# Alternating convolution taps, and the channel norm moved beside the last gate units, in a three-layer fp32 kernel

## The chip, the cores and the metric

The kernel runs on one core of a Trainium2 chip. The metric is device microseconds for one launch, the median of three runs. One more execution was taken with the hardware profiler; all trace rows are from it. "PE" is TensorE, "DVE" VectorE, "ACT" ScalarE, "SP" the queue that issues the weight loads.

## The reference, cut to what matters

256 tokens of width 2048 pass through two blocks of layers, in fp32. The change touches only the first ("even") layer:

```python
def _conformer_conv(a_val, a_gt, w_dw, b_dw, ln_g, ln_b, w_pw, b_pw):
    u = a_val * jax.nn.sigmoid(a_gt)
    y = lax.conv_general_dilated(u, w_dw[:, None, :], ...) + b_dw      # depthwise, 31 taps, causal
    y = jax.nn.silu(_layernorm(y, ln_g, ln_b))                         # over 1024 channels
    return y @ w_pw + b_pw

def _even_layer(x, norm_g, w_in, b_glu, w_dw, b_dw, ln_g, ln_b, w_pw, b_pw, w_out):
    z = _rmsnorm(x, norm_g) @ w_in
    a_val, a_gt, a_gate, q, k, v, b_gate = _split_cols(z, ...)
    ya = _conformer_conv(...) * jax.nn.silu(a_gate)
    yb = _moba_attention(q, k, v) * jax.nn.silu(b_gate)                # 8 heads, causal, one block of 256
    return jnp.concatenate([ya, yb], axis=-1) @ w_out
```

## The kernel before, in words

Activations lie transposed: channels on partitions, in tiles of 128 channels by 256 tokens. Each matrix is worked off in units of 128 output channels ("narrow" units), or, for `e_v` and `e_out`, in "wide" units that are a quarter of the contraction for 512 output columns. The segments of the first layer, in order: `e_gt`, `e_val`, `e_k`, `e_q`, `e_v`, `e_bgate`, `e_agate`, `e_pw` (8 units each) and `e_out` (16).

Every fp32 weight is split in two parts. For each unit, ACT copies the loaded weight into one of four slots as `w_hi` (L1221, L1218), DVE subtracts it to give `w_lo` (L1821, L1817), and PE multiplies three combinations of hi and lo. So a unit n passes ACT, DVE and PE in this order, through semaphores `hi_ready`, `lo_ready` and `acc_ready`. ACT may write the slot of unit n only when PE has finished n-4. The results are drained with a lag of three: after splitting unit n, ACT drains unit n-3 and DVE posts unit n-3 (for "paired" segments an addition from PSUM, L1854; for `e_val` also the product with the sigmoid that gives `u`, L1859). PE has two result banks, so a paired unit n waits for the post of n-2. SP loads chunks of two units (four for `e_pw`) into a ring of two; a chunk's load waits until DVE has split the last unit of the chunk two earlier.

DVE's instructions are in one fixed order: per unit the split, the post, and then a hook for "beside" work. From `e_val` unit 4 to `e_bgate` unit 3 this hook makes the depthwise convolution (`conv_taps`, L2034): 8 tiles of 31 taps, tile after tile, in groups of eight or seven. Each tap reads and writes the same `conv` tile and waits on the semaphore `conv_tap` for the tap just before it.

Counting `e_bgate` and `e_agate` as units u = 0 to 15, the hooks `e_heads_beside` do the attention: on PE, scores of head u-1 (L784), transposes of head u-3 (L799), values of head u-4 (L789, L790), each after unit u; on DVE, mask and maximum of head u-4 (L2058, L2061), division by the sum for head u-5 (L2068, L2069, `p_ready`); on ACT, the exponentials of head u-4. PE's transposes of head 0 after unit 3 wait for `p_ready`.

After unit 13, PE sums the convolution over channels (`conv_mean`, L826). Behind the last gate unit come, one after another: DVE subtracts the mean (L2096), ACT squares (L1453), PE sums the squares (L834), ACT takes the root (L1456), DVE inverts (L2099) and multiplies (L2101), ACT makes eight `Silu` tiles (L1459), ACT copies the result as its hi part into `h_cat` (`h_round`, L1405) and DVE makes the lo part (`h_rest`, L1990). `h_cat` has 16 tiles and feeds every matmul. `e_pw` reads tiles 8 to 15. Its output `ya` goes to tiles 0 to 7, the attention's output `qe` to tiles 8 to 15, and `e_out` contracts over tiles 0 to 15 in this order.

Of the kernel before, what the change touches and what calls it, by code (L numbers as in the profile page):

```python
# [20 lines left out]
ALU = mybir.AluOpType  # L21
# [42 lines left out]
class Seg:  # L64


    def __init__(self, name, units, kt, staged=False, wide=False):
        self.name, self.units, self.kt, self.staged, self.wide = name, units, kt, staged, wide
        self.paired = staged or name in ("e_k", "e_q", "o_iq", "o_q", "g_c", "x_q", "x_k")
        self.kq = kt // 4  # L70
        self.k0 = 8 if name == "g_out" else 0
        self.per_chunk = 2 if wide else max(2, 2 * KT // kt)
# [144 lines left out]
def build(nc, a, out):  # L217
# [154 lines left out]
    def p_tile(a_):  # L372
# [8 lines left out]
             "ht_hi", "ht_ready", "tiles_read", "hhi_ready", "h_ready", "x_normed", "gain1_loaded", "gain_out_loaded",  # L381
# [24 lines left out]
    H_GROUPS = {"conv": 0, "ya": 2, "qe": 4, "cq": 6, "cq_again": 7, "gate": 8, "gdn": 12, "xattn": 16}  # L406
# [81 lines left out]
    def _(sp):  # L488
# [21 lines left out]
        for g in order:  # L510
            if g.name in ("o_small", "g_ab", "g_out"):
                for k in range(g.chunks):
                    load(g, k // 2, k % 2, False)
                continue
            for b in range(min(2, g.chunks)):
                load(g, 0, b, False)
            if g is order[0]:
                for row in other_tables:
                    load_rows(sp, row, "tables_loaded")
            if g.chunks > 2:  # L520
                with sp.Fori(1, g.chunks // 2) as i:
                    for b in range(2):
                        load(g, i, b, True)
# [128 lines left out]
    def _(pe):  # L652
# [150 lines left out]
        def e_heads_beside(u0):  # L803

            def also(j):
# [16 lines left out]
                if u_ == 13:  # L822
                    pe.wait_ge(sem["conv_tap"], TAPS * CT)
                    pe.wait_ge(sem["masked"], HEADS)
                    for c in range(CT):
                        ins = mm(ps[2][:, 0:T], ones[:], conv[:, c, :], start=(c == 0), stop=(c == CT - 1))  # L826
                    ins.then_inc(sem["conv_mean"], 1)
            return also

        seg("e_bgate", also=e_heads_beside(0))  # L830
        seg("e_agate", also=e_heads_beside(8))
        pe.wait_ge(sem["conv_sq"], 1)
        for c in range(CT):
# [366 lines left out]
    def _(act):  # L1200
# [22 lines left out]
        def drain(g, n, i=None):  # L1223
# [16 lines left out]
            elif g.name == "e_bgate":  # L1240
                act.wait_ge(sem["conv_tap"], TAPS * (CT if j == 7 else CT - 1))
# [196 lines left out]
        def e_heads_beside(u0):  # L1438
            def also(i, b):
                u_ = u0 + 4 * i + b  # L1440
                if 4 <= u_ < 4 + HEADS:
                    exp_step(u_ - 4)
                if 6 <= u_ < 6 + HEADS:
                    h = u_ - 6
                    pt_step(h, pe_pt, ps[4 + h % 2], sem["o_ready"], h)
            return also

        seg("e_bgate", e_heads_beside(0))
        seg("e_agate", e_heads_beside(8))

        act.wait_ge(sem["conv_centred"], 1)
        act.wait_ge(sem["o_ready"], HEADS)
        af(csq[:], conv[:], ACT.Square).then_inc(sem["conv_sq"], 1)  # L1453
        section("e_pw")
        act.wait_ge(sem["conv_var"], 1)
        af(rstd[:], ps[3][:, 0:T], ACT.Sqrt, bias=eps[:], scale=1.0 / CW).then_inc(sem["conv_std"], 1)  # L1456
# [3 lines left out]
        h_round(H_GROUPS["conv"], 2, lambda q: conv[:, 4 * q:4 * q + 4], lambda q: act.wait_ge(sem["conv_silu"], 4 * q + 4), CT)  # L1460

        def ya_round(q):

            h_round(H_GROUPS["ya"] + q, 1, lambda _: ya[:, 4 * q:4 * q + 4],
                    lambda _: act.wait_ge(sem["posted"], S["e_pw"].s0 + 4 * q + 4), 4 * q)

        seg("e_pw", lambda i, b: ya_round(0) if 4 * i + b == 7 else None)
        split_to(S["e_out"].n0 + 1)
        drain_to(S["e_out"].n0)
        ya_round(1)  # L1470
        act.wait_ge(sem["acc_ready"], S["e_pw"].n0 + 8)
        act.wait_ge(sem["o_drained"], HEADS)
        h_round(H_GROUPS["qe"], 2, lambda q: qe[:, 4 * q:4 * q + 4], lambda q: None, CT)
# [327 lines left out]
    def _(dve):  # L1801
# [216 lines left out]
        def conv_taps(tile0):  # L2018

            def also(i, b):  # L2020
                if tile0 < 0 and isinstance(i, int) and i == 0:
                    return
                c = tile0 + i
                if tile0 < 0 and b == 0:
                    dve.wait_ge(sem["posted"], S["e_val"].s0 + 1)
                for tap in range(8 * b, min(8 * b + 8, TAPS)):
                    o = flat(conv[:, bass.ds(c, 1), :])
                    win = flat(u[:, bass.ds(c, 1), tap:tap + T])
                    w = prm[:, bass.ds(c + COL["dw"] + tap * CT, 1)]
                    if tap == 0:  # L2030
                        ins = nc.vector.tensor_scalar(o, win, w, col("b_dw", c), ALU.mult, ALU.add)
                    else:
                        dve.wait_ge(sem["conv_tap"], c * TAPS + tap)
                        ins = stt(o, win, w, o, ALU.mult, ALU.add)  # L2034
# [3 lines left out]

        seg("e_val", conv_taps(-1))
        seg("e_k", conv_taps(1))  # L2040
        seg("e_q", conv_taps(3))
        e_v_taps = conv_taps(5)
# [29 lines left out]
        def e_heads_beside(u0):  # L2072
            taps = conv_taps(CT - 1)

            def also(i, b):
# [7 lines left out]
                if 7 <= u_ < 7 + HEADS:  # L2083
# [3 lines left out]
                    tt(qe[:, h, :], ps[6 + h % 2][:, 0:T], bg[:, h, :], ALU.mult).then_inc(sem["o_drained"], 1)  # L2087
            return also
# [4 lines left out]
        dve.wait_ge(sem["conv_mean"], 1)  # L2093
        ch.link(nc.vector.tensor_scalar(psq[:], ps[2][:, 0:T], 1.0 / CW, None, ALU.mult))
        mean = psq[:].unsqueeze(1).to_broadcast([P, CT, T])
        tt(conv[:], conv[:], mean, ALU.subtract).then_inc(sem["conv_centred"], 1)  # L2096
        section("e_pw")
        dve.wait_ge(sem["conv_std"], 1)
        ch.link(nc.vector.reciprocal(rstd[:], rstd[:]))  # L2099
        dve.wait_ge(sem["conv_centred"], 1)  # L2100
        tt(conv[:], conv[:], rstd[:].unsqueeze(1).to_broadcast([P, CT, T]), ALU.mult).then_inc(sem["conv_normed"], 1)  # L2101
        for q in range(2):
            h_rest(H_GROUPS["conv"], q, conv[:, 4 * q:4 * q + 4], CT)
        seg("e_pw", lambda i, b: h_rest(H_GROUPS["ya"], 0, ya[:, 0:4]) if 4 * i + b == 7 else None)
# [436 lines left out]
```

## Time and profile before

| | us |
|---|---|
| median of 3 runs (2612.84 to 2614.36) | 2613.91 |
| the profiled execution, its own time | 2616.9 |
| its span, first to last instruction | 2615.1 |
| PE busy in the span | 2500.4 (96%) |
| DVE busy | 1642.1 (63%) |
| ACT busy | 1181.6 (45%) |

The span is the part that the trace shows; the execution's own time is 1.8 us more. Busy shares are means over the whole kernel, and a matmul's end is modelled, so a stage must be read by the starts of its instructions and by what an engine waited for. Times in rows are microseconds from the span's start.

### The profile page before, as it was taken

The page shows a single profiled execution, that of the slowest core. Times are in us where ns is not written, and L with a number is a line of the kernel's source. Part 1 is how long each engine was busy: PE and PEld are TensorE (multiplying, and loading weights), DVE is VectorE, ACT ScalarE, POOL GpSimd, SP SyncE. Part 2 cuts the span into 40 slices and gives each one's busy share as a digit, 9 for nine tenths or more (in the row PEclk, how much of TensorE's full clock was granted, in tenths as well). Part 3 has the DMA queues.
Part 4 walks back from the last instruction along what each step waited for, and adds up shares of the span by engine and source line. Part 5 has one row for each costly group of instructions (what it writes and reads, how often), then busy time and mean ns, then how long its engine had stood idle before and what let it go on. Part 6 is the DMA issues. An engine that isn't in the chain of part 4 may idle for free.

```text
span 2615.1 us, 35941 instructions
## 1 busy us (share of the span) xinstructions
PE 2500.4 (96%) x14366; PEld 2181.3 (83%) x14366; DVE 1642.1 (63%) x1941; ACT 1181.6 (45%) x1374; POOL 151.2 (6%) x136
## 2 busy tenths in 40 slices
PE   6999897999998999999999999999999999999998
PEld 6878896898887788988887888888888888888886
DVE  4799746445666578479466544554677657765764
ACT  5333655444455554454235434433555334333433
POOL 0000000000110010000000000000022102210220
PEclk9999998999999999999999999999999999999999
DMA  7444433644333555555006555444455555555544
GB/s 232 161 161 161 161 129 130 210 130 161 121 103 121 187 161 162 192 163 187 7 1 225 189 178 197 158 146 161 161 193 192 192 186 181 181 193 193 193 163 143
DMA packets 341284, 422.91 MB, mean 162 GB/s; under 512 B 14491, under 2 KB 267178, under 8 KB 340394
## 3 DMA queue, kind: packets, MB, share of 16 engines
q1 hardware_dynamic: 338620, 411.66, 47.4%
q0 software_dynamic: 2160, 8.40, 1.0%
q8 instruction: 91, 1.49, 0.2%
q10 hardware_dynamic: 382, 1.11, 0.1%
q14 instruction: 31, 0.25, 0.0%
HBM read 419.05 MB, written 2.10 MB: 161 GB/s over the span
## 4 chain that ended last, share of the span: by engine, by line
PE 84%; DVE 12%; ACT 3%; issue 1%; DMA 1%; ACTq 0%; DVEq 0%
PE ps L678 25%; PE ps L679 13%; PE ps L723 8%; PE ps L725 8%; PE ps L724 8%; DVE conv L2034 4%; PE ps L681 4%; PE ps L682 4%; PE ps L683 4%; DVE w_lo L1821 3%; PE ps L944 3%; DVE w_lo L1817 1%; PE ps L754 1%; PE ps L912 1%; PE ps L885 1%
## 5 line engine op out<-in xcount | busy, mean ns | idle before, releaser
L678 PE MATMUL ps<-h_cat,w_hi 128*128 128x512 f32 x3200 | 1143.7, 402 | 34.1 <-DVE h_cat L1990 14.1
L679 PE MATMUL ps<-h_cat,w_lo 128*128 128x256 f32 x3200 | 900.2, 281 | 0.0
L1821 DVE TENSOR_TENSOR w_lo<-ring,w_hi 128x2048 fp32r<-128x2048 f32 (+2 forms) x282 | 592.1, 2102 | 280.9 <-ACT w_hi L1221 277.8
L678 PEld LDWEIGHTS ps<-h_cat,w_hi 128*128 128x128 f32 x3200 | 603.8, 189 | 191.7 <-DVE w_lo L1821 22.0
L679 PEld LDWEIGHTS ps<-h_cat,w_lo 128*128 128x128 f32 x3200 | 607.3, 190 | 2.1 <-issue 1.9
L1221 ACT ACTIVATE w_hi<-ring 128x2048 fp32r<-128x2048 f32 (+2 forms) x282 | 495.5, 1760 | 118.9 <-PE ps L725 74.8
L1817 DVE TENSOR_TENSOR w_lo<-ring,w_hi 128x2048 fp32r<-128x2048 f32 (+1 forms) x136 | 302.9, 2232 | 232.2 <-ACT w_hi L1218 232.2
L1218 ACT ACTIVATE w_hi<-ring 128x2048 fp32r<-128x2048 f32 (+1 forms) x136 | 252.3, 1862 | 291.2 <-PE ps L725 250.8
L723 PE MATMUL ps<-w_hi,h_cat 128*128 128x512 f32 x704 | 277.5, 394 | 7.7 <-DVE w_lo L1817 4.8
L725 PE MATMUL ps<-w_hi,h_cat 128*128 128x512 f32 x704 | 275.7, 392 | 0.0
L724 PE MATMUL ps<-w_lo,h_cat 128*128 128x512 f32 x704 | 275.5, 391 | 0.0
L681 PE MATMUL ps<-h_cat,w_hi 128*128 128x256 f32 (+2 forms) x928 | 267.8, 289 | 7.1 <-DVE w_lo L1821 6.2
L682 PE MATMUL ps<-h_cat,w_hi 128*128 128x256 f32 (+2 forms) x928 | 263.7, 284 | 0.0
L683 PE MATMUL ps<-h_cat,w_lo 128*128 128x256 f32 (+2 forms) x928 | 263.6, 284 | 0.0
L1235 ACT ACTIVATE stage<-ps 128x256 f32<-128x256 f32 x144 | 55.4, 384 | 429.5 <-PE ps L679 429.5
L681 PEld LDWEIGHTS ps<-h_cat,w_hi 128*128 128x128 f32 (+2 forms) x928 | 174.7, 188 | 12.8 <-DVE w_lo L1821 8.4
L682 PEld LDWEIGHTS ps<-h_cat,w_hi 128*128 128x128 f32 (+2 forms) x928 | 174.7, 188 | 1.3
L683 PEld LDWEIGHTS ps<-h_cat,w_lo 128*128 128x128 f32 (+2 forms) x928 | 174.6, 188 | 1.2
L723 PEld LDWEIGHTS ps<-w_hi,h_cat 128*128 128x128 f32 x704 | 133.2, 189 | 36.4 <-DVE w_lo L1817 5.6
L725 PEld LDWEIGHTS ps<-w_hi,h_cat 128*128 128x128 f32 x704 | 133.1, 189 | 27.8
L724 PEld LDWEIGHTS ps<-w_lo,h_cat 128*128 128x128 f32 x704 | 133.3, 189 | 27.5
L723 PE MATMUL ps<-w_hi,act_cat 128*128 128x512 f32 x352 | 137.0, 389 | 0.0
(381 smaller groups left out, 2482.7 us busy)
## 6 DMA issues: line engine op xcount, KB each, us to landing
ring<-in_w_ffn_up SPq DMA_DIRECT2D x44, 2048.0 KB, 7.9
ring<-in_even_w_in SPq DMA_DIRECT2D x28, 2048.0 KB, 7.9
ring<-in_w_mix_in SPq DMA_DIRECT2D x28, 2048.0 KB, 7.9
ring<-in_w_ffn_down SPq DMA_DIRECT2D x16, 2048.0 KB, 8.0
ring<-in_odd_w_in SPq DMA_DIRECT2D x11, 2048.0 KB, 8.1
ring<-in_even_w_out SPq DMA_DIRECT2D x8, 2048.0 KB, 8.2
ring<-in_odd_w_out SPq DMA_DIRECT2D x8, 2048.0 KB, 8.0
ring<-in_w_mix_out SPq DMA_DIRECT2D x8, 2048.0 KB, 8.0
```

What stands on the lines that cost most here:

```text
L678: mm(o[:, 0:2 * T], whi[slot][:, k, :], flat(cat[:, k]), start=first, stop=False)
L679: ins = mm(o[:, T:2 * T], wlo[slot][:, k, :], cat[:, k, 0, :], start=False, stop=end)
L681: mm(o[:m, 0:T], whi[slot][:, k, 0:m], cat[:, k, 0, :], start=first, stop=False)
L682: mm(o[:m, 0:T], whi[slot][:, k, 0:m], cat[:, k, 1, :], start=False, stop=False)
L683: ins = mm(o[:m, 0:T], wlo[slot][:, k, 0:m], cat[:, k, 0, :], start=False, stop=end)
L723: mm(o[:], cat[:, k, 0, toks], hi, start=first, stop=False)
L724: mm(o[:], cat[:, k, 0, toks], lo, start=False, stop=False)
L725: ins = mm(o[:], cat[:, k, 1, toks], hi, start=False, stop=end)
L1218: af(flat(whi[slot])[:, 0:size], flat(ring[c % RING])[:, u0:u0 + size], ACT.Copy).then_inc(sem["hi_ready"], 1)
L1221: af(whi[slot][:, 0:g.kt, 0:m], chunk(c % RING, g)[:, :, u0:u0 + m], ACT.Copy).then_inc(sem["hi_ready"], 1)
L1817: tt(flat(wlo[slot])[:, 0:size], flat(ring[c % RING])[:, u0:u0 + size], flat(whi[slot])[:, 0:size].bitcast(F32), ALU.subtract).then_inc(se ...
L1821: tt(wlo[slot][:, 0:g.kt, 0:m], chunk(c % RING, g)[:, :, u0:u0 + m], whi[slot][:, 0:g.kt, 0:m].bitcast(F32), ALU.subtract).then_inc(sem["l ...
```

## The change

Taps: `conv_taps` now numbers all 248 taps, and alternates between two tiles (tap 0 of tile 0, tap 0 of tile 1, tap 1 of tile 0, ...). Tap n waits only for tap n-2, the last one on its own tile. The number of taps per unit is 7 in `e_val` (units 4 to 7), `e_k` and `e_q`, 8 in `e_v`, 11 in `e_bgate` units 0 to 3 (before: 8, 8, 8, 7 repeating). The DVE segments `e_val`, `e_k`, `e_q` and ACT's two gate segments are written out instead of looped.

Norm: the channel sum moves from behind unit 13 to behind unit 11, the sum of squares behind unit 12. Subtraction and squares are made by DVE and ACT at their own u = 14, root, inverse and product at u = 15. The `Silu` tiles stand between the drains of `e_agate`'s units 5 and 6, and the hi copies follow PE's last gate unit quarter by quarter (new semaphore `agate_read`), with the `e_pw` weight splits between them. The convolution goes to tiles 0 to 7 of `h_cat`, and `e_pw` waits for each half of them.

Output: `e_out` contracts tiles 8 to 15 first (`k0 = 8`). `qe` is written into `h_cat` in the first units of `e_pw`; both halves of `ya` are written when `e_pw` is over, after three units of `e_out` have been split.

```diff
--- before.py
+++ after.py
@@ -68,7 +68,7 @@
         self.name, self.units, self.kt, self.staged, self.wide = name, units, kt, staged, wide
         self.paired = staged or name in ("e_k", "e_q", "o_iq", "o_q", "g_c", "x_q", "x_k")
         self.kq = kt // 4
-        self.k0 = 8 if name == "g_out" else 0
+        self.k0 = 8 if name in ("e_out", "g_out") else 0
         self.per_chunk = 2 if wide else max(2, 2 * KT // kt)
 
 
...
@@ -403,7 +403,7 @@
         ends[c] = g.n0 + min(g.per_chunk * (j + 1), g.units)
     seg_of_unit = {g.n0 + j: (g, j) for g in order for j in range(g.units)}
     seg_of_narrow = {g.f0 + j: (g, j) for g in order if not g.wide for j in range(g.units)}
-    H_GROUPS = {"conv": 0, "ya": 2, "qe": 4, "cq": 6, "cq_again": 7, "gate": 8, "gdn": 12, "xattn": 16}
+    H_GROUPS = {"conv": 0, "qe": 2, "ya": 4, "cq": 6, "cq_again": 7, "gate": 8, "gdn": 12, "xattn": 16}
     SQUARES = {0: 8, 1: 16, 2: 32, 4: 40, 3: 48, 5: 56, 6: 64}
 
     def width(g, j):
@@ -508,7 +508,7 @@
                 sp.dma_start(chunk(slot, g)[:, :, cols], src).then_inc(loaded[slot], 16)
 
         for g in order:
-            if g.name in ("o_small", "g_ab", "g_out"):
+            if g.name in ("o_small", "g_ab", "e_out", "g_out"):
                 for k in range(g.chunks):
                     load(g, k // 2, k % 2, False)
                 continue
@@ -819,23 +819,23 @@
                     if h >= 2:
                         pe.wait_ge(sem["o_drained"], h - 1)
                     e_values(h, h).then_inc(sem["o_ready"], 1)
-                if u_ == 13:
+                if u_ == 11:
                     pe.wait_ge(sem["conv_tap"], TAPS * CT)
                     pe.wait_ge(sem["masked"], HEADS)
                     for c in range(CT):
                         ins = mm(ps[2][:, 0:T], ones[:], conv[:, c, :], start=(c == 0), stop=(c == CT - 1))
                     ins.then_inc(sem["conv_mean"], 1)
+                if u_ == 12:
+                    pe.wait_ge(sem["conv_sq"], 1)
+                    for c in range(CT):
+                        ins = mm(ps[3][:, 0:T], ones[:], csq[:, c, :], start=(c == 0), stop=(c == CT - 1))
+                    ins.then_inc(sem["conv_var"], 1)
             return also
 
         seg("e_bgate", also=e_heads_beside(0))
-        seg("e_agate", also=e_heads_beside(8))
-        pe.wait_ge(sem["conv_sq"], 1)
-        for c in range(CT):
-            ins = mm(ps[3][:, 0:T], ones[:], csq[:, c, :], start=(c == 0), stop=(c == CT - 1))
-        ins.then_inc(sem["conv_var"], 1)
-        pe.wait_ge(sem["h_ready"], H_GROUPS["conv"] + 2)
-        seg("e_pw", rhs=h_cat[:, CT:])
-        wide_seg("e_out", tiles_ready=H_GROUPS["ya"])
+        seg("e_agate", also=e_heads_beside(8), read="agate_read")
+        seg("e_pw", tiles_ready=H_GROUPS["conv"])
+        wide_seg("e_out", tiles_ready=H_GROUPS["qe"])
         turn_first(1)
         seg("o_small", norm=1)
 
@@ -1238,7 +1238,7 @@
             elif g.name in ("e_k", "e_q"):
                 ins = af({"e_k": ke, "e_q": qe}[g.name][:, at_j, :].rearrange("p a t -> p (a t)"), src, ACT.Copy)
             elif g.name == "e_bgate":
-                act.wait_ge(sem["conv_tap"], TAPS * (CT if j == 7 else CT - 1))
+                act.wait_ge(sem["conv_tap"], 2 * TAPS * (j // 2 + 1))
                 ins = af(bg[:, at_j, :].rearrange("p a t -> p (a t)"), src, ACT.Silu)
             elif g.name == "e_agate":
                 ins = af(ag[:, at_j, :].rearrange("p a t -> p (a t)"), src, ACT.Silu)
@@ -1443,34 +1443,57 @@
                 if 6 <= u_ < 6 + HEADS:
                     h = u_ - 6
                     pt_step(h, pe_pt, ps[4 + h % 2], sem["o_ready"], h)
+                if u_ == 14:
+                    act.wait_ge(sem["conv_centred"], 1)
+                    act.wait_ge(sem["o_ready"], HEADS)
+                    af(csq[:], conv[:], ACT.Square).then_inc(sem["conv_sq"], 1)
+                if u_ == 15:
+                    act.wait_ge(sem["conv_var"], 1)
+                    af(rstd[:], ps[3][:, 0:T], ACT.Sqrt, bias=eps[:], scale=1.0 / CW).then_inc(sem["conv_std"], 1)
             return also
 
-        seg("e_bgate", e_heads_beside(0))
-        seg("e_agate", e_heads_beside(8))
-
-        act.wait_ge(sem["conv_centred"], 1)
-        act.wait_ge(sem["o_ready"], HEADS)
-        af(csq[:], conv[:], ACT.Square).then_inc(sem["conv_sq"], 1)
-        section("e_pw")
-        act.wait_ge(sem["conv_var"], 1)
-        af(rstd[:], ps[3][:, 0:T], ACT.Sqrt, bias=eps[:], scale=1.0 / CW).then_inc(sem["conv_std"], 1)
+        seg("e_bgate", e_heads_beside(0), unrolled=True)
+        seg("e_agate", e_heads_beside(8), unrolled=True)
+
+        agate, pw, e_out = S["e_agate"], S["e_pw"], S["e_out"]
+        split_to(pw.n0 + 1)
+        drain_to(agate.n0 + 6)
         act.wait_ge(sem["conv_normed"], 1)
         for c in range(CT):
             af(conv[:, c, :], conv[:, c, :], ACT.Silu, bias=col("cln_b", c), scale=col("cln_g", c)).then_inc(sem["conv_silu"], 1)
-        h_round(H_GROUPS["conv"], 2, lambda q: conv[:, 4 * q:4 * q + 4], lambda q: act.wait_ge(sem["conv_silu"], 4 * q + 4), CT)
+        drain_to(agate.n0 + 7)
+
+        def conv_round(q):
+
+            act.wait_ge(sem["agate_read"], q + 1)
+            h_round(H_GROUPS["conv"] + q, 1, lambda _: conv[:, 4 * q:4 * q + 4],
+                    lambda _: act.wait_ge(sem["conv_silu"], 4 * q + 4), 4 * q)
+
+        def qe_round(q):
+
+            if q == 0:
+                act.wait_ge(sem["acc_ready"], agate.n0 + 8)
+                act.wait_ge(sem["o_drained"], HEADS)
+            h_round(H_GROUPS["qe"] + q, 1, lambda _: qe[:, 4 * q:4 * q + 4], lambda _: None, CT + 4 * q)
 
         def ya_round(q):
 
+            if q == 0:
+                act.wait_ge(sem["acc_ready"], pw.n0 + 8)
             h_round(H_GROUPS["ya"] + q, 1, lambda _: ya[:, 4 * q:4 * q + 4],
-                    lambda _: act.wait_ge(sem["posted"], S["e_pw"].s0 + 4 * q + 4), 4 * q)
-
-        seg("e_pw", lambda i, b: ya_round(0) if 4 * i + b == 7 else None)
-        split_to(S["e_out"].n0 + 1)
-        drain_to(S["e_out"].n0)
+                    lambda _: act.wait_ge(sem["posted"], pw.s0 + 4 * q + 4), 4 * q)
+
+        split_to(pw.n0 + 2)
+        conv_round(0)
+        split_to(pw.n0 + 3)
+        conv_round(1)
+        section("e_pw")
+        seg("e_pw", lambda i, b: qe_round(4 * i + b - 1) if 4 * i + b in (1, 2) else None)
+        for j in range(3):
+            split_to(e_out.n0 + j + 1)
+            drain_to(pw.n0 + 6 + j)
+        ya_round(0)
         ya_round(1)
-        act.wait_ge(sem["acc_ready"], S["e_pw"].n0 + 8)
-        act.wait_ge(sem["o_drained"], HEADS)
-        h_round(H_GROUPS["qe"], 2, lambda q: qe[:, 4 * q:4 * q + 4], lambda q: None, CT)
         wide_seg("e_out", lambda c: squares(S["e_out"], c))
         section("o_small", 3)
         table_for_roots()
@@ -2015,31 +2038,28 @@
         turned_rows(0, x)
         seg("e_gt", tables_beside, unrolled=True)
 
-        def conv_taps(tile0):
+        def conv_taps(first, per_unit, from_unit=0):
 
             def also(i, b):
-                if tile0 < 0 and isinstance(i, int) and i == 0:
-                    return
-                c = tile0 + i
-                if tile0 < 0 and b == 0:
-                    dve.wait_ge(sem["posted"], S["e_val"].s0 + 1)
-                for tap in range(8 * b, min(8 * b + 8, TAPS)):
-                    o = flat(conv[:, bass.ds(c, 1), :])
-                    win = flat(u[:, bass.ds(c, 1), tap:tap + T])
-                    w = prm[:, bass.ds(c + COL["dw"] + tap * CT, 1)]
+                at = 4 * i + b - from_unit
+                for n in range(first + at * per_unit, min(first + (at + 1) * per_unit, CT * TAPS)) if at >= 0 else ():
+                    two, tap = n // (2 * TAPS), n % (2 * TAPS) // 2
+                    c = 2 * two + n % 2
+                    o, win = conv[:, c, :], u[:, c, tap:tap + T]
+                    w = prm[:, c + COL["dw"] + tap * CT:c + COL["dw"] + tap * CT + 1]
                     if tap == 0:
+                        dve.wait_ge(sem["posted"], S["e_val"].s0 + c + 1)
                         ins = nc.vector.tensor_scalar(o, win, w, col("b_dw", c), ALU.mult, ALU.add)
                     else:
-                        dve.wait_ge(sem["conv_tap"], c * TAPS + tap)
+                        dve.wait_ge(sem["conv_tap"], n - 1)
                         ins = stt(o, win, w, o, ALU.mult, ALU.add)
                     ins.then_inc(sem["conv_tap"], 1)
             return also
 
-
-        seg("e_val", conv_taps(-1))
-        seg("e_k", conv_taps(1))
-        seg("e_q", conv_taps(3))
-        e_v_taps = conv_taps(5)
+        seg("e_val", conv_taps(0, 7, 4), unrolled=True)
+        seg("e_k", conv_taps(28, 7), unrolled=True)
+        seg("e_q", conv_taps(84, 7), unrolled=True)
+        e_v_taps = conv_taps(140, 8)
         g = S["e_v"]
         for j in range(g.units):
             split_to(g.n0 + j + 1)
@@ -2070,7 +2090,7 @@
                ALU.mult).then_inc(sem["p_ready"], 1)
 
         def e_heads_beside(u0):
-            taps = conv_taps(CT - 1)
+            taps = conv_taps(204, 11)
 
             def also(i, b):
                 u_ = u0 + 4 * i + b
@@ -2085,28 +2105,35 @@
                     dve.wait_ge(sem["o_ready"], h + 1)
                     dve.wait_ge(*emptied(S["e_bgate"], h + 1))
                     tt(qe[:, h, :], ps[6 + h % 2][:, 0:T], bg[:, h, :], ALU.mult).then_inc(sem["o_drained"], 1)
+                if u_ == 14:
+                    dve.wait_ge(sem["conv_mean"], 1)
+                    ch.link(nc.vector.tensor_scalar(psq[:], ps[2][:, 0:T], 1.0 / CW, None, ALU.mult))
+                    mean = psq[:].unsqueeze(1).to_broadcast([P, CT, T])
+                    tt(conv[:], conv[:], mean, ALU.subtract).then_inc(sem["conv_centred"], 1)
+                if u_ == 15:
+                    dve.wait_ge(sem["conv_std"], 1)
+                    ch.link(nc.vector.reciprocal(rstd[:], rstd[:]))
+                    dve.wait_ge(sem["conv_centred"], 1)
+                    tt(conv[:], conv[:], rstd[:].unsqueeze(1).to_broadcast([P, CT, T]), ALU.mult)\
+                        .then_inc(sem["conv_normed"], 1)
             return also
 
         seg("e_bgate", e_heads_beside(0), unrolled=True)
         seg("e_agate", e_heads_beside(8), unrolled=True)
 
-        dve.wait_ge(sem["conv_mean"], 1)
-        ch.link(nc.vector.tensor_scalar(psq[:], ps[2][:, 0:T], 1.0 / CW, None, ALU.mult))
-        mean = psq[:].unsqueeze(1).to_broadcast([P, CT, T])
-        tt(conv[:], conv[:], mean, ALU.subtract).then_inc(sem["conv_centred"], 1)
+        pw, e_out = S["e_pw"], S["e_out"]
+        split_to(pw.n0 + 2)
+        h_rest(H_GROUPS["conv"], 0, conv[:, 0:4])
+        split_to(pw.n0 + 3)
+        h_rest(H_GROUPS["conv"], 1, conv[:, 4:8])
         section("e_pw")
-        dve.wait_ge(sem["conv_std"], 1)
-        ch.link(nc.vector.reciprocal(rstd[:], rstd[:]))
-        dve.wait_ge(sem["conv_centred"], 1)
-        tt(conv[:], conv[:], rstd[:].unsqueeze(1).to_broadcast([P, CT, T]), ALU.mult).then_inc(sem["conv_normed"], 1)
+        seg("e_pw", lambda i, b: h_rest(H_GROUPS["qe"], 4 * i + b - 1, qe[:, 16 * i + 4 * b - 4:16 * i + 4 * b], CT)
+            if 4 * i + b in (1, 2) else None)
+        for j in range(3):
+            split_to(e_out.n0 + j + 1)
+            post_to(pw.n0 + 6 + j)
         for q in range(2):
-            h_rest(H_GROUPS["conv"], q, conv[:, 4 * q:4 * q + 4], CT)
-        seg("e_pw", lambda i, b: h_rest(H_GROUPS["ya"], 0, ya[:, 0:4]) if 4 * i + b == 7 else None)
-        split_to(S["e_out"].n0 + 1)
-        post_to(S["e_out"].n0)
-        h_rest(H_GROUPS["ya"], 1, ya[:, 4:8])
-        for q in range(2):
-            h_rest(H_GROUPS["qe"], q, qe[:, 4 * q:4 * q + 4], CT)
+            h_rest(H_GROUPS["ya"], q, ya[:, 4 * q:4 * q + 4])
         wide_seg("e_out", lambda c: add(S["e_out"], c))
         section("o_small", 3)
         add(S["e_out"], 3)
```

## Rows read from the trace of the kernel before

**Rows 1.** Stretches: length, busy us (instructions) of each engine, TensorE's granted clock, DMA share, GB/s.
```profile
40.72:75.28 34.56, 34.56 (x291) 34.56 (x289) 16.23 (x15) 13.64 (x12) 0.00 (x0) 1.00 0.71 232
75.28:97.89 22.61, 22.61 (x131) 19.60 (x129) 15.67 (x23) 8.85 (x8) 0.00 (x0) 1.00 0.43 137
412.44:426.57 14.13, 14.13 (x83) 12.26 (x81) 10.66 (x15) 7.96 (x11) 0.00 (x0) 1.00 0.10 27
454.11:519.39 65.28, 65.28 (x289) 54.05 (x288) 33.31 (x19) 26.67 (x24) 0.00 (x0) 1.00 0.58 196
97.89:269.25 171.36, 159.96 (x834) 133.46 (x832) 164.85 (x258) 59.24 (x50) 0.00 (x0) 1.00 0.49 164
269.25:312.19 42.94, 36.00 (x269) 34.92 (x269) 34.03 (x48) 28.28 (x34) 0.00 (x0) 0.92 0.49 159
389.88:407.43 17.55, 3.44 (x17) 2.67 (x16) 11.03 (x8) 13.13 (x18) 0.00 (x0) 0.74 0.35 120
407.43:454.11 46.68, 43.27 (x200) 36.00 (x201) 28.12 (x30) 21.60 (x22) 0.00 (x0) 0.91 0.37 131
```

**Rows 2.** What PE waited for, 75.28 to 454.11: total us, times, longest.
```profile
PE ps L678 <- DVE h_cat L1990: 14.1, 1, 14.1
PE ps L799 <- DVE pe_p L2069: 6.8, 1, 6.8
...
PE ps L723 <- DVE w_lo L1817: 3.1, 1, 3.1
```

**Rows 3.** Timeline of DVE, `e_val` and `e_k` taps: start, length of the merged group, instruction.
```profile
129.57 0.48 DVE L1859 SCALAR_TENSOR_TENSOR u<-stage,prm,sig 128x256 f32<-128x256 f32 x1
129.97 4.13 DVE L2034 SCALAR_TENSOR_TENSOR conv<-u,prm,conv 128x256 f32<-128x256 f32 x8
134.01 2.28 DVE L1821 TENSOR_TENSOR w_lo<-ring,w_hi 128x2048 fp32r<-128x2048 f32 x1
...
136.55 3.60 DVE L2034 SCALAR_TENSOR_TENSOR conv<-u,prm,conv 128x256 f32<-128x256 f32 x7
```

**Rows 4.** Timeline of DVE, four independent instructions of the tap's kind and shape.
```profile
593.70 1.67 DVE L2128 SCALAR_TENSOR_TENSOR cq<-cq,prm,orq 128x256 f32<-128x256 f32 x4
```

**Rows 5.** Timeline of DVE, the first head: mask, the next split, the division.
```profile
293.49 0.68 DVE L2058 SCALAR_TENSOR_TENSOR pe_p<-ps,causal 128x512 f32<-128x512 f32 x1
...
297.86 2.29 DVE L1821 TENSOR_TENSOR w_lo<-ring,w_hi 128x2048 fp32r<-128x2048 f32 x1 [2.96 <-ACT w_hi L1221]
300.07 0.68 DVE L2058 SCALAR_TENSOR_TENSOR pe_p<-ps,causal 128x512 f32<-128x512 f32 x1
...
301.58 0.69 DVE L2069 TENSOR_TENSOR pe_p<-pe_p,small 128x512 f32<-128x512 f32 x1
```

**Rows 6.** Timeline of PE behind one gate unit: scores, transposes, values, next unit.
```profile
318.03 1.03 PE L784 MATMUL ps<-ke,qe 128*128 128x256 f32 x4
318.90 0.60 PE L799 MATMUL ps<-ident,pe_p 128*128 128x128 f32 x4
319.33 0.60 PE L789 MATMUL ps<-pe_pt,ve 128*128 128x256 f32 x2
...
319.91 0.36 PE L681 MATMUL ps<-h_cat,w_hi 128*128 128x256 f32 x1
```

**Rows 7.** Timeline of DVE and ACT, the channel norm.
```profile
378.86 2.29 DVE L2096 TENSOR_TENSOR conv<-conv,psq 128x2048 f32<-128x2048 f32 x1
...
381.18 1.91 ACT L1453 ACTIVATE csq<-conv 128x2048 f32<-128x2048 f32 x1 [11.61 <-DVE conv L2096]
...
395.89 1.75 DVE L2099 RECIPROCAL rstd<-rstd 128x256 f32<-128x256 f32 x1
...
400.00 4.04 ACT L1459 ACTIVATE conv<-conv,prm 128x256 f32<-128x256 f32 x8 [2.85 <-DVE conv L2101]
...
405.01 2.36 DVE L1990 TENSOR_TENSOR h_cat<-conv,h_cat 128x1024 fp32r<-128x1024 f32 x2 [5.05 <-ACT h_cat L1405]
```

**Rows 8.** The page, part 6, weight loads: KB each, median us to landing.
```profile
ring<-in_even_w_out SPq DMA_DIRECT2D x8, 2048.0 KB, 8.2
```

More of the change, by code:

```diff
@@ L380, in build @@
              "row_ready", "emptied", "squared", "gained", "totalled", "std_ready", "rstd_ready", "scaled_dve", "scaled_act", "turned",
-             "ht_hi", "ht_ready", "tiles_read", "hhi_ready", "h_ready", "x_normed", "gain1_loaded", "gain_out_loaded",
+             "ht_hi", "ht_ready", "tiles_read", "agate_read", "hhi_ready", "h_ready", "x_normed", "gain1_loaded", "gain_out_loaded",
              "conv_tap", "conv_mean", "conv_centred", "conv_sq", "conv_var", "conv_std", "conv_normed", "conv_silu",
```

## The prediction

> **What bounds the kernel now.** I read the stretches with their granted clock first, then PE's waits, then the timelines of DVE, PE and ACT at the places found. The stretches come first, since a matmul's busy time is modelled and only the starts of units tell its pace. Where PE never waits, a unit has a fixed pace [rows 1]: 34.56 us for six unpaired units of `e_gt`, 5.76 each; 22.61 for four paired of `e_val`, 5.65 each; 14.13 for five of `e_pw`, 2.83 each; 65.28 for twelve wide ones of `e_out`, 5.44 each. Those are the first four rows; PE is busy throughout and the clock is 1.00. The other four rows are longer than their units need. From 97.89 to 269.25 PE does 4 + 8 + 8 paired and 8 wide units, 20 x 5.65 + 8 x 5.44 = 156.6, but takes 171.4, with DVE busy 164.9 of it: DVE bounds this stretch. In the next two stretches and the last, PE waits for something that was late: for `pe_p` of the first head (6.8), for `h_cat` of the convolution (14.1), for one `w_lo` (3.1) [rows 2]. Each of those waits is followed by a spell at half clock, seen as 0.92, 0.74 and 0.91 in the stretches. So the first layer is PE's wherever DVE or a serial chain isn't late, and the change aims at all four places. From 454.11 on nothing is changed; the rest moves as a block.
>
> **The price of a tap.** A merged group of eight dependent taps lasts 4.13 us, one instruction 0.485, so the pitch is (4.13 - 0.485) / 7 = 0.52 us; the whole group up to the next start is 134.01 - 129.97 = 4.04, so the last, with nothing dependent behind it, takes 0.40 [rows 3]. Four independent instructions of the same kind and shape last 1.67, a pitch of (1.67 - 0.48) / 3 = 0.40 [rows 4]. They overlap; dependent ones don't, and wait some 0.04 for the semaphore too. With two tiles alternating, tap n needs the end of tap n-2, which started 0.80 earlier and lasts 0.485: satisfied. I take 0.40 a tap; the bounds are 0.40 and 0.52 (no effect). 248 taps x 0.12 = 30 us of DVE time.
>
> The Trainium skill, page "VectorE: DVE Perf Modes", section "The DRAIN you can't avoid", speaks against this: the next op does not start until the pipe is empty and the semaphore costs nothing, so one should cut the number of ops, not the waits. By it the taps would stay at 0.52. The rows above say otherwise for this shape, and I go by them.
>
> **DVE-bound stretch, 97.89 to 269.25.** New DVE time a unit: split and paired post 136.55 - 134.01 = 2.54 [rows 3], 7 taps 2.8, so 5.36 in `e_k` and `e_q` against PE's 5.65: PE is the bound, DVE waits. `e_val` units add the 0.40 of `u` (129.57 to 129.97): 5.76 to 5.9, four times 0.1 to 0.2 over PE's pace, covered by the post's slack (the post of n-3 is due only when PE has finished n-2, a unit later). `e_v`: split 2.21 (297.86 to 300.07, [rows 5]) + 8 x 0.40 = 5.4 against 5.44. The ring: a load needs 8.2 [rows 8] after DVE's split, and its next use is two units (10.9 to 11.3) on, plus DVE's lead; covered, with 3 us to spare, and without cover each chunk would cost what is missing. Saved: 171.4 - 156.6 = **14.8**.
>
> **First head, 269.25 to 312.19.** Five gate units need 28.8, plus scores 0.87, transposes 0.43, values 0.58 [rows 6]: behind u = 1 and 2 scores, u = 3 scores and transposes, u = 4 all three, 2 x 0.87 + 1.30 + 1.88 = 4.9. 33.7 instead of 42.9, if `p_ready` is in time. That is the tight place. While paired units run, DVE's post ties it to PE: split n+1 starts about 3.8 after PE ends n-3 (0.7 for the drain, an estimate from the 0.33 post of the same shape, then 0.33 and 2.8), 13.2 before PE begins n+1. Over `e_v`, with three last posts, DVE takes 44.4 to PE's 43.5: lead 12.3. `e_bgate` units 0 to 3 have eleven taps, 2.21 + 4.4 = 6.6 each: the split of unit 4 starts 14.3 after PE's start of unit 0. From there 2.2 to the mask, 4.4 from mask to the next split (293.49 to 297.86, the exponentials and ACT's copy inside), 2.2 to the next mask, 2.2 to the end of the product [rows 5]: 25.3. PE arrives at 4 x 5.76 + 3 x 0.87 = 25.65. The margin is 0.3 us; each 0.01 on the tap's pitch takes about 1 us (64 + 44 taps where DVE sets the pace). At 0.40 saved: **9.2**; I allow 0.5 for a slip.
>
> **Norm chain, 389.88 to 407.43.** All of the 17.55 goes but the sum of squares, 3.3 on PE (its 3.44 busy), which must be done somewhere: **14.3**. The cover: with zero at the end of unit 11, values and mean end at 3.9; mean copy and subtraction to 6.8, squares (1.9) to 8.8, and PE finishes unit 12 at 3.9 + 5.76 = 9.7, margin 0.9. Sum of squares to 12.9; root, then inverse, product (395.89 to 400.00, 4.1) to 17.8. `Silu` stands behind the drain of unit 13, which PE ends at 18.7: 19.3 + 4.0 = 23.3 [rows 7]. Unit 15 starts at 24.4 and ends at 30.2; hi and lo of the first half (1.0 and 1.2) follow its first quarter, and the `e_pw0` split is long done, so `e_pw` may start at 30.2 with about 2 us in hand; its second half is needed 1.4 later and comes at about 30.7. Behind ACT's waits for the norm stand only splits of `e_pw`, due at 30 or later.
>
> **`e_pw` and the start of `e_out`, 407.43 to 454.11.** 46.7 against 8 x 2.83 + 3 x 5.44 = 38.9: **7.7**, of which 2.2 is `e_pw0` at half clock, 5.0 the late `w_lo` of `e_out1` and the half clock behind it. `e_out0` and 1 now read `qe`, copied during `e_pw`. With zero at the start of `e_pw`, the load for `e_out2` goes out at 14.1, lands at 22.9, is split by 27, posts and both `ya` halves end at 30.4; `e_out2` starts at 33.5. Margin 3 us. The three units' splits are done before `ya`, so the old gap has no successor I can see. ACT and DVE segments written out instead of looped: no cost, as `e_v` and the gates are already so on DVE and show no gaps; a bound above is nothing that a row shows.
>
> **Sum.** 14.8 + 9.2 + 14.3 + 7.7 = 46.0, less 0.5: 45.5. On the profiled execution: 2616.9 - 45.5 = 2571.4, span 2569.6. That execution is 3.0 over the median; on the median 2613.9 - 45.5 = **2568.4 us**.
>
> **Rivals.**
> (a) Head 0 late: a tap's pitch of 0.42 to 0.46, or a slower exponential. PE waits 2 to 7 us at the transposes; waits of 3 us and more were followed by half clock, so 2571 to 2579. For: the margin is 0.3. Against: 0.397 in [rows 4], 0.40 before every split. Chance 0.17.
> (b) Norm or ring late: one of the waits in ACT's or DVE's new order comes late by more than its margin, worst one whole landing (8.2): 2571 to 2578. For: ACT's order is now full of waits for PE. Against: margins of 1 to 3 us. Chance 0.13.
> (c) Alternation gives nothing, pitch 0.52. DVE does the same work to `e_bgate` 3, head 0 is as late as before; only norm and output gain, 22.0: 2592. This is what the page's rule above comes to. Chance 0.05.
> (d) Slower than before: two interleaved streams on different `u` and `conv` tiles make each tap dearer. DVE then pays 248 x (p - 0.52), and the 22 us are eaten at p = 0.61; at 0.65 the time is 2624. No row shows such an instruction over 0.52. Chance 0.02. No change at all would need p at just about 0.61: 0.01.
> The forecast case, 2565 to 2572, has the remaining 0.62.
>
> **How the numbers follow.** 2568 is the likeliest. The range 2564 to 2581 holds the forecast and nearly all of (a) and (b), about 0.9, less what later stages may do (half-clock spells behind 454 fall where they fall, a few us); (c) and (d) are outside. About 0.2% (5 us) is what a measurement here can tell from no change. Faster by more: (forecast), (a), (b), (c): 0.97; within 0.01; slower 0.02.
>
> **What would show it.** Taps of a group at 0.40 from start to start; 156 us from `e_val4` to `e_bgate0`, with no PE wait for `ke`, `qe` or `stage`; transposes of head 0 without a wait; `e_pw0` right behind `e_agate` 7; no half clock between 75 us and `o_small`. PE waits for `pe_p` at 280 us would mean (a), for `h_cat` or `w_lo` at 369 to 410 (b), taps at 0.52 (c). The prediction is wrong if a stage I took for PE's turns out to wait for ACT, whose new order has more waits for PE than any stretch of the profile before.

## The result, and the profile after

The changed kernel takes 2565.74 us (median of 4 runs, 2565.47 to 2569.22), the kernel before 2614.14 (4 runs, 2612.84 to 2614.85). The ratio is 0.9821, 95% interval 0.9809 to 0.9833: 48.4 us saved. The forecast was 2568.4, 45.5 saved, range 2564 to 2581.

The stretches of the changed kernel, cut at the same units as [rows 1]: `e_val4` to `e_bgate0`, to `e_bgate5`, to `e_pw0`, to `e_out0`, to `e_out3`, and from there to the end. Columns: stretch, length, busy us (instructions) of PE, PE's weight loads, DVE, ACT and POOL, granted clock, DMA share, GB/s.

```profile
97.73:254.35 156.62, 156.62 (x835) 134.14 (x834) 153.67 (x265) 61.00 (x52) 0.00 (x0) 1.00 0.56 186
254.35:288.04 33.69, 33.69 (x270) 33.11 (x268) 25.87 (x39) 22.51 (x29) 0.00 (x0) 1.00 0.51 163
288.04:369.00 80.96, 80.96 (x632) 79.14 (x630) 46.59 (x48) 55.55 (x75) 0.00 (x0) 1.00 0.39 131
369.00:391.61 22.61, 22.61 (x131) 19.60 (x129) 19.02 (x24) 13.78 (x18) 0.00 (x0) 1.00 0.55 186
391.61:407.99 16.38, 16.38 (x74) 13.51 (x73) 12.39 (x9) 9.16 (x7) 0.00 (x0) 1.00 0.71 243
407.99:2563.70 2155.71, 2098.19 (x11887) 1821.72 (x11885) 1312.76 (x1494) 966.56 (x1138) 149.08 (x126) 0.99 0.50 162
```

In the first five rows PE's busy time is the length of the stretch and the clock is 1.00. The view of PE's waits from 75 to 410 us, which had the rows of [rows 2] in the kernel before, is empty. Against [rows 1]: 156.6 for 171.4, 33.7 for 42.9, 39.0 (22.61 + 16.38) for 46.7; and `e_agate` 7 ends where `e_pw0` starts. `e_val4` to `e_out3` took 454.11 - 97.89 = 356.2 us and now takes 310.3, 46.0 less.

DVE's timeline in `e_k`, and where the first head begins (`w_lo` is L1844 now, the tap L2055, mask L2078, maximum L2081, product L2089):

```profile
125.48 2.29 DVE L1844 TENSOR_TENSOR w_lo<-ring,w_hi 128x2048 fp32r<-128x2048 f32 x1
127.69 0.41 DVE L1877 TENSOR_TENSOR ke<-ke,ps 128x256 f32<-128x256 f32 x1
128.02 2.86 DVE L2055 SCALAR_TENSOR_TENSOR conv<-u,prm,conv 128x256 f32<-128x256 f32 x7
130.79 2.28 DVE L1844 TENSOR_TENSOR w_lo<-ring,w_hi 128x2048 fp32r<-128x2048 f32 x1
...
263.61 4.44 DVE L2055 SCALAR_TENSOR_TENSOR conv<-u,prm,conv 128x256 f32<-128x256 f32 x11
267.97 2.29 DVE L1844 TENSOR_TENSOR w_lo<-ring,w_hi 128x2048 fp32r<-128x2048 f32 x1
270.17 0.69 DVE L2078 SCALAR_TENSOR_TENSOR pe_p<-ps,causal 128x512 f32<-128x512 f32 x1
...
278.26 0.69 DVE L2089 TENSOR_TENSOR pe_p<-pe_p,small 128x512 f32<-128x512 f32 x1
```

Seven taps last 2.86, a pitch of (2.86 - 0.48) / 6 = 0.397, where [rows 3] had 0.52; a unit takes DVE 5.31 (125.48 to 130.79) against PE's 5.65. The product of head 0 ends at 278.95. PE's timeline there:

```profile
279.10 1.03 PE L784 MATMUL ps<-ke,qe 128*128 128x256 f32 x4
279.96 0.60 PE L799 MATMUL ps<-ident,pe_p 128*128 128x128 f32 x4
```

The transposes start at 279.96, with no wait: the product (278.26 + 0.69 = 278.95) was ready 1.0 us before.

The norm chain after, on ACT (squares L1449, root L1452, `Silu` L1463, hi copies L1405) and on DVE (subtraction L2112, inverse L2115, lo parts L2013):

```profile
345.51 1.92 ACT L1449 ACTIVATE csq<-conv 128x2048 f32<-128x2048 f32 x1 [6.51 <-DVE conv L2112]
...
351.93 0.47 ACT L1452 ACTIVATE rstd<-ps,eps 128x256 f32<-128x256 f32 x1 [1.14 <-PE ps L831]
...
357.96 4.03 ACT L1463 ACTIVATE conv<-conv,prm 128x256 f32<-128x256 f32 x8
...
364.88 1.06 ACT L1405 ACTIVATE h_cat<-conv 128x1024 fp32r<-128x1024 f32 x1
```

```profile
352.44 1.75 DVE L2115 RECIPROCAL rstd<-rstd 128x256 f32<-128x256 f32 x1 [0.89 <-ACT rstd L1452]
...
365.97 1.22 DVE L2013 TENSOR_TENSOR h_cat<-conv,h_cat 128x1024 fp32r<-128x1024 f32 x1
367.12 1.22 DVE L1844 TENSOR_TENSOR w_lo<-ring,w_hi 128x1024 fp32r<-128x1024 f32 x1
368.25 1.22 DVE L2013 TENSOR_TENSOR h_cat<-conv,h_cat 128x1024 fp32r<-128x1024 f32 x1
```

ACT and DVE still wait in this chain, but PE doesn't. The squares end at 347.4, and PE starts its sum of squares (L831) at 348.3, right behind unit 12. The two halves for `e_pw` are ready at 367.2 and 369.5; `e_pw0` starts at 369.0 and needs the second half a unit, 1.4 us, later.

### The profile page after: what moved, and what is told of

The parts are those of the page before. It is cut to its first block, busy times and chain, and to the rows that moved or that the text cites. A ratio compares the mean times of both kernels' runs of the same rounds, so it can differ in the third digit from the quotient of the medians.

```text
span 2563.7 us, 35901 instructions
## 1 busy us (share of the span) xinstructions
PE 2486.2 (97%) x14366; PEld 2175.2 (85%) x14366; DVE 1622.7 (63%) x1941; ACT 1176.6 (46%) x1371; POOL 151.1 (6%) x136
## 4 chain that ended last, share of the span: by engine, by line
PE 94%; DVE 4%; ACT 2%; issue 0%; DMA 0%; ACTq 0%; DVEq 0%
PE ps L678 29%; PE ps L679 15%; PE ps L723 9%; PE ps L725 9%; PE ps L724 9%; PE ps L681 4%; PE ps L682 4%; PE ps L683 4%; PE ps L944 3%; PE ps L754 1%; DVE w_lo L1844 1%; PE ps L912 1%; PE ps L885 1%; PE ps L1141 1%; PE ps L1132 1%; PE ps L901 0%
## 5 line engine op out<-in xcount | busy, mean ns | idle before, releaser
L1844 DVE TENSOR_TENSOR w_lo<-ring,w_hi 128x2048 fp32r<-128x2048 f32 (+2 forms) x282 | 592.3, 2102 | 278.6 <-ACT w_hi L1221 275.6
```

What stands on the lines that cost most here:

```text
L1844: tt(wlo[slot][:, 0:g.kt, 0:m], chunk(c % RING, g)[:, :, u0:u0 + m], whi[slot][:, 0:g.kt, 0:m].bitcast(F32), ALU.subtract).then_inc(sem["l ...
```

## The experiments

**Only the taps, `e1_taps_only`.** The kernel before with the new `conv_taps`, its spread and the written-out segments:

```diff
-        seg("e_k", conv_taps(1))
+        seg("e_k", conv_taps(28, 7), unrolled=True)
...
-                        dve.wait_ge(sem["conv_tap"], c * TAPS + tap)
+                        dve.wait_ge(sem["conv_tap"], n - 1)
```

> Only the alternating taps (with their new spread over the units); norm chain, places in h_cat and order of e_out as before. My theory: the four places are independent, each gives back its own idle time. Taps at a pitch of 0.40, 97.9 to e_bgate0 in 156.6 us, head 0 in time, together 24.0 us: about 2590. The gap behind e_agate 7 stays at 17.5. Rival (the places share a cause, so that an earlier PE only meets the norm chain's wait earlier and longer): the gap behind e_agate 7 grows and less than 20 us is saved.

Measured: 2589.46 us, ratio to before 0.9903 (0.9885 to 0.9921), 25.1 less than before's median of 2614.57 in these runs. Its stretches `e_val4` to `e_bgate0`, to `e_bgate5`, end of `e_agate` 7 to `e_pw0`, and on to `e_out3`:

```profile
97.31:253.93 156.62, 156.62 (x835) 134.03 (x833) 153.70 (x265) 61.02 (x52) 0.00 (x0) 1.00 0.56 186
253.93:287.62 33.69, 33.69 (x270) 33.11 (x268) 25.88 (x39) 22.50 (x29) 0.00 (x0) 1.00 0.51 162
365.31:382.85 17.54, 3.43 (x16) 2.66 (x16) 11.03 (x8) 13.13 (x18) 0.00 (x0) 0.71 0.36 121
382.85:428.79 45.94, 42.42 (x201) 35.58 (x201) 27.90 (x30) 21.59 (x22) 0.00 (x0) 0.92 0.39 136
```

The first two stretches are the changed kernel's, the last two the old ones (17.54 for 17.55, 45.9 for 46.7). The gap behind the gates did not grow, and more than 20 us were saved, so the rival falls. From `e_val4` to `e_out3` it saves 24.7 us in the trace.

**Only norm and output, `e2_norm_output_only`.** The changed kernel with the old `conv_taps` and its loops.

```diff
-                        dve.wait_ge(sem["conv_tap"], n - 1)
+                        dve.wait_ge(sem["conv_tap"], c * TAPS + tap)
```

> The moved norm, the new places in h_cat and the order of e_out, with the taps tile after tile as before. My theory: taps stay at 0.52, the DVE-bound stretch stays at 171.4 and head 0 as late as before; norm and output give 14.3 + 7.7 = 22.0, about 2592. Rival (the norm beside the gates needs a DVE that is ahead): the sum of squares or e_pw0 waits some us, 2594 to 2600.

Measured: 2591.90 us, ratio 0.9917 (0.9900 to 0.9934), 22.7 less. Its stretches to `e_bgate0`, to `e_bgate5`, and `e_pw0` to `e_out3`:

```profile
97.07:268.48 171.41, 160.04 (x834) 133.58 (x832) 164.90 (x258) 59.14 (x50) 0.00 (x0) 1.00 0.50 164
268.48:311.02 42.54, 35.61 (x269) 34.53 (x269) 33.63 (x48) 25.20 (x32) 0.00 (x0) 0.92 0.50 161
391.99:430.98 38.99, 38.99 (x202) 33.12 (x201) 31.33 (x32) 22.95 (x24) 0.00 (x0) 1.00 0.58 197
```

The tap stretches are the old ones, the last is the new one, and `e_pw0` starts 5.76 behind the start of `e_agate` 7, without a gap. From `e_bgate5` to `e_pw0` it takes 80.97 us (311.02 to 391.99), against 80.96 in the changed kernel: the moved norm needs no DVE that is ahead, so the rival falls. From `e_val4` to `e_out3` it saves 22.3. By the traces the two parts save 24.7 + 22.3 = 47.0 us there, the whole change 46.0; by the medians it is 25.1 + 22.7 = 47.8 against 48.4.

**The same taps with the stricter wait, `e3_wait_for_last_tap`.** One line of the changed kernel:

```diff
-                        dve.wait_ge(sem["conv_tap"], n - 1)
+                        dve.wait_ge(sem["conv_tap"], n)
```

> The changed kernel, but each tap waits for the tap just before it, which is of the other tile, instead of for the one two before. Data, order and spread of the taps are those of the changed kernel. My theory (the gain comes from not waiting for the previous instruction's end): pitch 0.52, DVE bounds the stretch again, about 2592. Rival (the semaphore costs nothing, what counts is whether the data depend): pitch 0.40, as the changed kernel, 2566.

Measured: 2590.42 us, ratio 0.9912 (0.9895 to 0.9928). DVE's timeline in `e_k`:

```profile
131.63 0.41 DVE L1877 TENSOR_TENSOR ke<-ke,ps 128x256 f32<-128x256 f32 x1
131.97 3.60 DVE L2055 SCALAR_TENSOR_TENSOR conv<-u,prm,conv 128x256 f32<-128x256 f32 x7
135.48 2.29 DVE L1844 TENSOR_TENSOR w_lo<-ring,w_hi 128x2048 fp32r<-128x2048 f32 x1
```

Instructions, tiles and order are those of the changed kernel; only the count waited for differs. Seven taps last 3.60 instead of 2.86: the pitch is 0.52 again. So a wait for the instruction just before is enough to cost 0.12 a tap, though no data pass between the two. No run has dependent data without such a wait, so whether the dependence alone would cost anything isn't shown. Its stretches to `e_bgate0` and to `e_bgate5`:

```profile
96.54:260.36 163.82, 159.83 (x834) 133.56 (x832) 157.96 (x245) 59.05 (x50) 0.00 (x0) 1.00 0.52 172
260.36:309.80 49.44, 37.68 (x268) 36.05 (x269) 40.07 (x61) 25.25 (x32) 0.00 (x0) 0.86 0.42 134
```

Together they take 213.3 us, against 214.3 with the old taps [rows 1] and 190.3 in the changed kernel. With fewer taps early and eleven behind each of four gate units, the first stretch is shorter and the second longer; the sum hardly moves, since DVE does the same 248 taps at the same pitch. That also settles two rivals: written-out segments and the new spread are in this kernel too, and without the looser wait they save 1.0 us in the two stretches, where the whole change saves 24.0.

**A late first head, `e4_late_head_4` and `e5_late_head_12`.** Four or twelve more linked instructions on DVE behind the last taps:

```diff
                 if u_ < 4:
                     taps(0, b)
+                if u_ == 3:
+                    for _ in range(4):
+                        ch.link(stt(psq[:], causal[:, 0, :], eps[:], causal[:, 0, :], ALU.mult, ALU.add))
```

> The changed kernel with four more linked DVE instructions of the tap's kind (0.52 each, 2.1 us) behind the taps of e_bgate unit 3. They write a scratch tile. In the trace of the changed kernel p_ready comes 1.0 us before PE's transposes of head 0. If that is the margin: PE waits 1.1 us there, no half clock, 1 us slower than the changed kernel, and nothing else moves. Rival (DVE catches up inside the head's chain, so the margin is larger): no wait.

> The same with twelve such instructions, 6.2 us. Theory: PE waits 5.2 us at head 0's transposes, and a spell of half clock follows as after the 6.8 us of the kernel before (some 1.5 to 3 us more): 6.7 to 8 us slower than the changed kernel. Rival (the spell of half clock needs more than this wait): 5.2 us slower and the clock at 1.00.

Each ran once, with 2569.99 and 2574.41 us, 1.0 and 5.4 more than the changed kernel's execution beside them (`a1_after_again`, 2569.03). Single executions can't carry differences of this size, so the traces decide. PE's timeline at the transposes of head 0, of the first and then of the second:

```profile
280.12 0.66 PE L799 MATMUL ps<-ident,pe_p 128*128 128x128 f32 x4 [0.96 <-DVE pe_p L2089]
```

```profile
284.67 1.11 PE L799 MATMUL ps<-ident,pe_p 128*128 128x128 f32 x4 [5.12 <-DVE pe_p L2089]
```

2.1 us more work give a wait of 0.96, 6.2 us more give 5.12: the margin is 2.1 - 1.0 = 1.1 and 6.2 - 5.1 = 1.1 us. From `e_val4` to `e_out3` the two take 311.4 and 317.0 us, 1.2 and 6.7 more than the changed kernel. Behind the short wait the units keep their pace. Behind the long one the next unit takes 8.71 instead of 7.71, at a mean clock of 0.87, that is, in part at half clock. So the theory of `e5_late_head_12` (6.7 to 8) holds at its lower end, and its rival (5.2, clock at 1.00) falls. Its stretches, `e_bgate0` to 4 and 4 to 5:

```profile
253.77:285.44 31.67, 26.55 (x210) 25.87 (x208) 27.36 (x46) 14.97 (x20) 0.00 (x0) 0.98 0.39 123
285.44:294.15 8.71, 8.71 (x62) 8.51 (x61) 4.66 (x6) 7.96 (x11) 0.00 (x0) 0.87 0.56 181
```

**The old order of k in `e_out`, `e6_ya_half_first`.** In the changed kernel:

```diff
-        self.k0 = 8 if name in ("e_out", "g_out") else 0
+        self.k0 = 8 if name == "g_out" else 0
...
-                            pe.wait_ge(sem["h_ready"], tiles_ready + step // 4 + 1)
+                            early = 2 if g.name == "e_out" else 0
+                            pe.wait_ge(sem["h_ready"], tiles_ready + min(step // 4 + early, 3) + 1)
```

> The changed kernel with e_out contracting tiles 0 to 15 in order again, so that its first unit waits for ya. My theory: PE ends e_pw at 391.6 and ya's halves are ready at about 397.3 and 398.5, so a wait of 5.7 us at e_out0, followed by half clock (1.5 to 2 more): about 2573. Rival (the splits of e_out1 and e_out2 were the bound and the order of k only moves the wait): no more than 2 us slower, 2566 to 2568.

Measured: 2575.70 us (2572.97 to 2578.03), ratio to before 0.9857 (0.9840 to 0.9874), so 10.0 slower than the changed kernel's median, more than the 7 expected. Its executions lie 5 us apart, and the profiled one is the quickest: 2572.97, 7.5 over the profiled execution of the changed kernel. What makes the rest of the 10.0 wasn't found. In the trace the loss is the expected one, and the rival (2 us at most) falls. PE's only wait from 75 to 415 us, and the stretches `e_pw0` to `e_out0` and `e_out0` to `e_out3`:

```profile
PE ps L724 <- DVE h_cat L2014: 5.6, 1, 5.6
```

```profile
368.60:396.95 28.35, 22.77 (x130) 19.51 (x129) 23.55 (x29) 17.59 (x22) 0.00 (x0) 0.94 0.62 214
396.95:415.06 18.11, 18.11 (x72) 14.83 (x73) 7.95 (x4) 5.45 (x3) 0.00 (x0) 0.90 0.39 131
```

46.5 instead of 39.0: 5.6 of waiting and 1.7 in slower units behind it, 7.5 in all.

**Both kernels again, `b1_before_again` and `a1_after_again`.**

> The kernel before, once more with a profile. The first 454 us should repeat within 0.3 us. Behind them the two profiled executions shown so far drew apart by 5 us more than the 46.1 of the first layer, with nothing changed there. If that is this execution's own slowness (2616.9 against a median of 2613.9), this one ends some 3 us earlier; if it is due to the change, it does not.

> The changed kernel, once more with a profile, beside the last: e_out3 starts 46.1 us earlier than in the kernel before, and behind it the two keep their distance within 3 us, half-clock spells falling where they fall.

One execution each: 2615.41 and 2569.03 us. Stretches from `e_val4` to `e_out3` and from there to the end, before and after:

```profile
97.37:452.96 355.59, 319.31 (x1930) 282.76 (x1929) 274.71 (x383) 166.30 (x182) 0.00 (x0) 0.97 0.46 152
452.96:2613.70 2160.74, 2101.50 (x11887) 1823.61 (x11885) 1315.28 (x1495) 966.57 (x1138) 149.11 (x126) 0.99 0.49 161
```

```profile
97.89:408.15 310.26, 310.26 (x1931) 279.50 (x1929) 257.43 (x382) 161.99 (x179) 0.00 (x0) 1.00 0.51 170
408.15:2567.30 2159.15, 2100.16 (x11887) 1821.89 (x11885) 1312.94 (x1494) 966.62 (x1138) 149.10 (x126) 0.99 0.49 162
```

The changed stretch repeats to the hundredth (310.26 twice); before it differs by 0.6 (356.22 and 355.59). `e_out3` starts at 452.96 instead of 454.11 in the kernel before, so the expectation of 0.3 for the repetition was missed by far, and in this pair the changed kernel reaches it 44.8 us earlier, not 46.1; behind it the two keep their distance within the 3 us expected. The unchanged rest took 2160.99 and 2160.74 before, 2155.71 and 2159.15 after. In this pair the rest accounts for 1.6 us, not 5.3. The execution before ended 1.5 us earlier than the first, not 3, and 1.15 of that lies ahead of `e_out3`: the kernel before shows the longer rest both times.

Between the two executions of the changed kernel the rest differs by 3.4 us. Laid beside each other instruction by instruction, they part mainly in one place, a stretch made up mostly of paired units. The same stretch of it, the first execution and then the second, and four units inside it:

```profile
868.97:1014.47 145.50, 145.50 (x879) 126.19 (x878) 113.09 (x160) 75.56 (x76) 9.96 (x22) 1.00 0.56 171
914.70:936.88 22.18, 22.18 (x130) 19.39 (x129) 17.45 (x25) 12.38 (x11) 0.00 (x0) 1.00 0.60 188
```

```profile
869.09:1017.36 148.27, 148.27 (x879) 127.68 (x878) 113.18 (x160) 75.67 (x77) 9.97 (x22) 1.00 0.55 168
915.79:938.40 22.61, 22.61 (x130) 19.61 (x129) 17.45 (x25) 12.39 (x12) 0.00 (x0) 1.00 0.59 185
```

With the same instructions, no wait of PE and the full clock in both, a unit took 5.55 us in one and the usual 5.65 in the other. That is 2.8 us between executions of one and the same kernel, so this part of the 5.3 isn't due to the change. What sets the pace there no view shows.

## Why the prediction was right

The start of a unit on PE is that of its first matmul; the DVE start of `e_bgate0`, used below, is that of its `w_lo`.

- **The DVE-bound stretch.** Forecast 14.8 saved, measured 171.36 - 156.62 = 14.7. The step from "independent instructions of this kind follow at 0.40" to "alternating taps do" held: 0.397. One and the same stream of taps ran at 0.397 and at 0.52 us, by the count waited for alone, and that was worth 213.3 - 190.3 = 23.0 us in the two stretches and 2590.42 - 2565.74 = 24.7 by the medians. The page "VectorE: DVE Perf Modes" of the Trainium skill, section "The DRAIN you can't avoid", says that the next op waits for an empty pipe and that a semaphore behind each op costs nothing extra; the same section adds that a next op that isn't held starts earlier, which the prediction passed over. The traces agree with the addition: the next tap starts 0.09 us before the last one ends (0.397 against 0.48). They don't contradict the sentence on signalling, since every tap signals here in both kernels. What cost 0.12 us is the wait on the last one, so for this shape the advice to cut ops and not waits, as the prediction put it, doesn't hold.
- **The first head.** Forecast 9.2 saved less 0.5 for a slip; measured 42.94 - 33.69 = 9.25 and no slip. The margin was forecast at 0.3 us and is 1.0 by the trace, 1.1 by two experiments. The lead of DVE came out at 254.35 - 241.73 = 12.6 (`e_bgate0` on PE and on DVE) instead of 12.3, DVE's four units with eleven taps took 267.97 - 241.73 = 26.2 instead of 26.6, and PE reaches the transposes 25.6 after the start of `e_bgate0`, as forecast. Rival (a) was the right place to fear: 2.1 us more on DVE are enough to open a wait.
- **The norm chain.** Forecast 14.3. The stretch behind `e_bgate5` was 77.69 + 17.55 = 95.2 up to `e_pw0` and is 80.96: 14.3 saved. Margins: squares 0.9 forecast and 0.9 found (347.4 to 348.3); first half for `e_pw` 2 and 1.8; second half due at 370.4, ready at 369.5, 0.9 in hand as forecast (30.7 against 31.6).
- **`e_pw` and `e_out`.** Forecast 7.7, measured 46.68 - 38.99 = 7.7. `ya` is ready at 396.05 + 2.44 = 398.5 and `e_out2`, its first reader, starts at 402.5: 4 us in hand, 3 forecast. Taking the order of k alone back costs 7.5 in the trace, so without the early `qe` half nearly nothing of this part would be left. That the two numbers are close is chance: the kernel before waited there for a `w_lo` (3.1) and had `e_pw0` at half clock, the experiment waits for `ya` (5.6). The forecast's own split of the 7.7 has only 2.2 + 5.0 = 7.2 in it.
- **Rivals.** (a) and (b) didn't come: no wait of PE in 310 us. (c) is what `e3_wait_for_last_tap` makes of the change: 2590, against 2592 forecast for it. (d) would have needed a pitch of 0.61, and no tap in any of the ten traces is that far behind the one before it within its group.
- **The sum.** 46.0 in the profiled stretch, forecast 46.0. The median fell by 48.4, 2.4 more. The term that was mis-sized is the unchanged rest, counted at zero: it was 5.3 us shorter in one pair of traces and 1.6 in the other. Over all ten traces of these kernels it took 2155.7 to 2161.0 us. Of the 5.3, 2.8 are the faster paired units that only one of the two executions of the changed kernel has, and so scatter, not the change. Whether the rest of it, 2.5 in this pair and 1.6 in the other, comes from the change stays open. That 45.5 lies so near 48.4 is owed to the mechanism for 46.0 us; the rest of the difference no term foresaw.

## What to carry to other kernels

On an engine that works through a long chain of short dependent instructions, look at the pitch from start to start of dependent and of independent ones: if they differ, interleave two chains and wait for the one before last. Then ask which wait the slow engine had been hiding; here the margin of the next consumer, the first head, could be worked out to within a microsecond (0.3 forecast, 1.0 found) by adding durations from the rows. A serial chain across three engines is best moved beside work that needs none of its results, and a contraction should begin with the operand that is ready first.

## What the runs showed of the hardware

- A `scalar_tensor_tensor` of 128x256 fp32 takes 0.48 us from start to end, but the next started 0.397 after it where it waited for the one before last; a wait for the last one moved this to 0.52.
- A wait of 0.96 us on TensorE cost about 1 us (1.2 to `e_out3`), and the units behind it kept their pace; one of 5.12 was followed by a unit at a mean clock of 0.87, and of its 6.7 us total cost some 1.6 came behind the wait.
- The same paired units of PE, without a wait and at the full clock, took 5.55 us each in one execution and 5.65 in another of the same kernel (22.18 and 22.61 for four).
- Two pairs of idle places, each pair removed by itself, added up to the whole within about a microsecond (25.1 + 22.7 against 48.4 by the medians, 24.7 + 22.3 against 46.0 in the traces).
